# Root of the head norms by ScalarE with a Newton step, fox norm weights in the copies, and query and block-score work inside the last projection group of a hybrid decoder trunk

## Chip, cores and metric

The kernel runs on one core of one Trainium2 chip. The metric is the device time of one execution in microseconds; the time before is the median of 3 runs, 1247.37 us (1247.21 to 1249.06).

## The reference, cut to what matters

The whole program is a two-layer decoder trunk for 256 positions of width 1024 in float32 (attention, dense SwiGLU, gated linear attention, a mixture of 8 experts). The change touches only the first part, between the combined input projection and the attention branches:

```
proj = rmsnorm(x) @ w_in        # 6 column groups: (kc vc ksl kwn) (vsl vwn gates f) qa qb kb vb
qa, ksl, kwn = rope(rmsnorm(head, norm weight))      # per head of 64: x * rsqrt(mean(x^2) + 1e-6) * g
k_cmp = rope(rmsnorm(compress(kc)));  v_cmp = compress(vc)       # 15 blocks
s_c = q . k_cmp / 8 -> softmax -> o_c                # block scores: 15 columns per head
qb, kb = rmsnorm(head, fox norm weight)              # forgetting attention, no rope
cum = cumsum(log_sigmoid(f + bias))                  # added to q.k as two more rows (66 instead of 64)
```

Then follow 18 units of attention (selected, window, fox branch) and the output projection.

## The kernel before

**Input projection.** Weights stream from HBM in units of 4 blocks of 128x512. ScalarE rounds a unit (`split`, L1174), VectorE forms the remainder (`split`, L1498), and TensorE multiplies each block three times (high by high, low, and low by high, L562 to L564) for two tiles of 128 positions. A column group is 8 blocks, that is two units and 48 products. A unit's products wait for VectorE's remainder (`w_lo`), and the next loads and roundings wait until TensorE has used earlier units (`units_used`). Groups alternate between banks 4/5 and 6/7; ScalarE copies each finished group from PSUM to `proj[cg]` with the row norm's root as scale (L1226).

**Order.** There is no planner: every engine has its instruction list written out by hand, and an engine does its list strictly in order. TensorE's list is: groups 0 and 1, turning of the compressed keys (L660), group 2, the 64 products of the compression (L670), turning of keys (L677), group 3, small products (L682, L684), group 4, small products (L691, L695), group 5, then turning of the queries (L706), the cumulative sum of the forget gates (L712 to L714), the block scores (L721, 15 columns each), turning of fox queries and keys (L734), turning of the block probabilities (L738), their products with the values (L742), and the attention loop: scores `qk` (L758, L760), `turn` of the probabilities (L768) and `pv` (L786). In the loop `qk` runs two units ahead.

**Head norms.** VectorE squares a projected group in SBUF (L1534), sums per head (L1535) and signals GpSimd, which computes scale and offset (L498) and raises to the power -0.5 (L499). VectorE then multiplies by the root (L1544) and by the norm weight (L1546) and, for queries and keys, applies the rotation (L1550 to L1553). Between these steps VectorE does unit splits. The compressed key follows the same route on 30 partitions.

**Tail of the preparation.** ScalarE copies turned queries (L1242) and fox rows (L1250) from PSUM, and computes the exponentials of the block scores (L1245); VectorE adds the gate sums (L1692, L1693), masks and normalizes the block scores (L1701 to L1711), copies them (L1715), and scales the block outputs (L1723). The first rowmax (L1730) and exponentials (L1259) of the attention loop come after.

## Time and profile before

| | us |
|---|---|
| median of 3 runs | 1247.37 (1247.21 to 1249.06) |
| span of the profiled execution, first to last instruction | 1243.7 |
| lowest run less that span (the profiled execution's own total is not listed) | 3.5 |
| PE, DVE, ACT, POOL busy in the span | 1225.3, 982.9, 808.2, 52.0 |
| input projection, preparation of attention | 8.8 to 101.1 |
| attention loop up to the output projection | 101.1 to 141.3 |

The profile lists one execution. A timeline row gives the start, the duration from the first to the end of the last instruction of a merged row, engine, source line and operation; TensorE's rows are pipelined, so one more instruction adds less than the duration of one. A row of a chain gives start, duration and the work that held the end at that time. The granted clock is 1.00 for 2.4 GHz and 0.50 for 1.2 GHz.

### The profile page before, as it was taken

Reading aid. Unit: us, or ns where it says so; the run is one execution under the profiler, and the core shown is the slowest. Engines: PE = TensorE matmul, PEld = TensorE weight load, DVE = VectorE, ACT = ScalarE, POOL = GpSimd, SP = SyncE. Lnnn points to the kernel's source line nnn. Section 1 sums busy time; section 2 is a strip of 40 time slices with the busy share of each in tenths; the row PEclk is TensorE's granted clock in tenths of the full one; section 3 lists DMA queues with packets and bytes.
Section 4 is the critical chain, followed back from the end, with each engine's and each line's share of the span. In section 5 each row is a group of like instructions: output and inputs, shape, how many; then the busy total and the mean of one; then the engine's idle time right before and its main releaser. Section 6 shows DMA issues by size and latency. Waiting matters only on the chain.

```text
span 1243.7 us, 16151 instructions
## 1 busy us (share of the span) xinstructions
PE 1225.3 (99%) x6016; PEld 1020.3 (82%) x6021; DVE 982.9 (79%) x945; ACT 808.2 (65%) x877; POOL 52.0 (4%) x52
## 2 busy tenths in 40 slices
PE   8999999999999999999999999999999999999997
PEld 6888888888889886888888888888888888888886
DVE  5887664544567558999889889989989989989896
ACT  6545464343366547777777777777777777777773
POOL 1120000000000001000000000000000000000200
PEclk9989999999999999999999999999999999999999
DMA  9730145544444344999999999999999999999992
GB/s 356 294 135 1 41 163 203 203 173 171 172 184 149 135 153 182 364 401 372 397 377 373 398 376 374 397 380 369 398 381 369 395 384 368 392 371 368 396 422 88
DMA packets 53000, 361.42 MB, mean 291 GB/s; under 512 B 6048, under 2 KB 6560, under 8 KB 10944
## 3 DMA queue, kind: packets, MB, share of 16 engines
q1 hardware_dynamic: 49872, 349.41, 72.7%
q0 software_dynamic: 3056, 11.02, 2.2%
q8 instruction: 50, 0.82, 0.2%
q14 instruction: 22, 0.18, 0.0%
HBM read 354.63 MB, written 5.77 MB: 290 GB/s over the span
## 4 chain that ended last, share of the span: by engine, by line
PE 90%; DVE 4%; DMA 1%; POOL 1%; issue 1%; SPq 1%; ACT 1%; another core or an unknown queue 0%; DVEq 0%
PE bank L564 27%; PE bank L562 27%; PE bank L563 27%; PE bank L1083 2%; DMA raw<-in_weights 1%; PE bank L786 1%; PE bank L758 1%; PE bank L942 1%; DVE low L1498 1%; POOL arena L499 1%; PE bank L768 1%; PE bank L572 1%; PE bank L1048 0%; PE bank L734 0%; PE bank L830 0%
## 5 line engine op out<-in xcount | busy, mean ns | idle before, releaser
L2064 DVE TENSOR_TENSOR low<-raw,whi 128x2048 fp32r<-128x2048 f32 x260 | 594.8, 2291 | 66.5 <-ACT whi L1432 59.2
L1432 ACT CAST whi<-raw 128x2048 fp32r<-128x2048 f32 x260 | 497.4, 1913 | 114.8 <-PE bank L564 114.1
L562 PE MATMUL bank<-whi,hT_hi 128*128 128x512 f32 (+1 forms) x1104 | 430.5, 390 | 1.6 <-DVE low L1567 1.1
L564 PE MATMUL bank<-whi,hT_lo 128*128 128x512 f32 (+1 forms) x1104 | 428.7, 388 | 0.0
L563 PE MATMUL bank<-low,hT_hi 128*128 128x512 f32 (+1 forms) x1104 | 428.1, 388 | 0.0
L562 PEld LDWEIGHTS bank<-whi,hT_hi 128*128 128x128 f32 x1104 | 207.3, 188 | 44.7 <-DVE hT_lo L1516 1.5
L564 PEld LDWEIGHTS bank<-whi,hT_lo 128*128 128x128 f32 x1104 | 207.2, 188 | 42.7
L563 PEld LDWEIGHTS bank<-low,hT_hi 128*128 128x128 f32 x1104 | 207.4, 188 | 41.6
L1498 DVE TENSOR_TENSOR low<-raw,whi 128x2048 fp32r<-128x2048 f32 x67 | 153.0, 2288 | 47.4 <-ACT whi L1174 47.3
L562 PE MATMUL bank<-whi,h_hi 128*128 128x512 f32 x440 | 181.1, 412 | 0.0
L564 PE MATMUL bank<-whi,h_lo 128*128 128x512 f32 x440 | 172.5, 392 | 0.0
L563 PE MATMUL bank<-low,h_hi 128*128 128x512 f32 x440 | 172.0, 391 | 0.0
L1174 ACT CAST whi<-raw 128x2048 fp32r<-128x2048 f32 x67 | 127.9, 1916 | 15.3 <-PE bank L564 10.8
L564 PEld LDWEIGHTS bank<-whi,h_lo 128*128 128x128 f32 x440 | 82.6, 188 | 17.9
L563 PEld LDWEIGHTS bank<-low,h_hi 128*128 128x128 f32 x440 | 83.1, 189 | 14.2
L562 PEld LDWEIGHTS bank<-whi,h_hi 128*128 128x128 f32 x440 | 82.7, 188 | 13.7
L1449 ACT ACTIVATE sg<-bank 128x256 f32<-128x256 f32 x88 | 33.9, 385 | 64.7 <-PE bank L564 64.7
L1282 ACT ACTIVATE sg<-bank,rstd 128x256 f32<-128x256 f32 x22 | 10.4, 474 | 98.4 <-PE bank L564 98.4
L1783 DVE SCALAR_TENSOR_TENSOR hact<-bank,rstd,sg 128x256 f32<-128x256 f32 x22 | 10.6, 484 | 57.7 <-ACT sg L1282 57.7
L1189 ACT ACTIVATE hT_hi<-bank,sml 128x128 fp32r<-128x128 f32 x80 | 22.1, 376 | 29.4 <-PE bank L572 29.4
L2069 DVE TENSOR_TENSOR h_lo<-bank,h_hi 128x256 fp32r<-128x256 f32 x88 | 36.7, 417 | 1.0 <-ACT h_hi L1436 1.0
L2081 DVE TENSOR_TENSOR hact<-sg,bank 128x256 f32<-128x256 f32 x88 | 36.4, 413 | 0.0
(303 smaller groups left out, 830.2 us busy)
## 6 DMA issues: line engine op xcount, KB each, us to landing
raw<-in_weights SPq DMA_DIRECT2D x327, 1024.0 KB, 5.8
sums<-ybuf POOLq DMA_DIRECT2D x7, 512.0 KB, 7.5
arena<-in_compress SPq DMA_DIRECT2D x1, 1088.0 KB, 15.6
x<-in_x SPq DMA_DIRECT2D x2, 512.0 KB, 5.2
raw<-in_weights SPq DMA_DIRECT2D x4, 256.0 KB, 5.7
raw<-in_weights SPq DMA_DIRECT2D x2, 512.0 KB, 7.8
tokens<-hng POOLq DMA_DIRECT2D x2, 512.0 KB, 3.4
out<-x SPq DMA_DIRECT2D x4, 256.0 KB, 3.3
```

What stands on the lines that cost most here:

```text
L562: mm(out_, a_hi, b_hi, start=start, stop=False)
L563: mm(out_, a_hi, b_lo, start=False, stop=False)
L564: return mm(out_, a_lo, b_hi, start=False, stop=stop)
L1083: last = nc.tensor.transpose(bank[2][:, j * P:(j + 1) * P], hact[:, (par + c) % 2, j * P:(j + 1) * P], ident)
L1174: nc.scalar.copy(whi[:, u % SPLIT, :, :], raw[:, u % RAW, :, :]).then_inc(S["w_hi"], 1)
L1189: A(hT_hi[:, k, cols], src[:, j * P:(j + 1) * P], ACT.Copy, scale=sml[:, gc:gc + 1])\
L1432: nc.scalar.copy(whi[:, u % SPLIT, :, :], raw[:, u % RAW, :, :]).then_inc(S["w_hi"], 1)
L1449: A(sg[:, (par + c) % 2, :], bank[(par + c) % 2][:, 0:CH], ACT.Silu).then_inc(S["m_silu"], 1)
L1498: V.tensor_tensor(low[:, u % RAW, :, :], raw[:, u % RAW, :, :], whi[:, u % SPLIT, :, :].bitcast(F32), ALU.subtract).then_inc(S["w_lo"], 1)
L2064: V.tensor_tensor(low[:, u % RAW, :, :], raw[:, u % RAW, :, :], whi[:, u % SPLIT, :, :].bitcast(F32), ALU.subtract).then_inc(S["w_lo"], 1)
L2069: V.tensor_tensor(h2_lo[:, (par + c) % 2, :], bank[2][:, 0:CH], h2_hi[:, (par + c) % 2, :].bitcast(F32), ALU.subtract).then_inc(S["m_h2T"], 1)
L2081: V.tensor_tensor(hact[:, (par + c) % 2, :], sg[:, (par + c) % 2, :], bank[(par + c) % 2][:, CH:2 * CH], ALU.mult).then_inc(S["m_hact"], 1)
```

## The change

- The squares of the head norms are taken by ScalarE from PSUM, with the row root as scale, ahead of the group's copy; VectorE only sums. ScalarE takes the square root (a new function there, which needs another table of functions than the exponential or the logarithm), and VectorE forms the reciprocal and one Newton step in four small instructions, plus one that prepares half of the mean. GpSimd no longer takes part.
- The fox norm weights go as per-partition scale into the copies of the turned rows, so VectorE's second full multiplication for fox queries and keys goes. The last two of the eight fox copies move from ScalarE to VectorE.
- TensorE turns the first half of the queries before group 5, the second half within it (before its block 2), and does cumulative sum, block scores and the turning of fox queries before its block 4. After group 5 remain the turning of fox keys and block probabilities. The products of block probabilities and values come after the scores of attention units 0 and 1.
- VectorE's list is reordered: gates and forget gates earlier, unit splits 10 to 14 at other places; cumulative sum and block scores move to banks 5 and 4.

The diff, cut to its core (waits of `qk` and `turn`, sizes, and the layout of the weights on the host are left out):

```diff
             norm(0)
-            for i, n in enumerate((8, 16, 16, 16)):
-                pool.wait_ge(S["head_ss"], i + 1)
-                inv_root(hrs[:, i, 0:n], hss[:, i, 0:n], HD, n, "head_rstd")
-                if i == 1:
-                    pool.wait_ge(S["kcmp_ss"], 1)
-                    inv_root(hrs[0:30, 4, 0:1], hss[0:30, 4, 0:1], HD, 1, "kcmp_rstd")
...
+                    if hooks is not None and k in hooks:
+                        hooks[k]()
                     if b % UB == 0:
                         pe.wait_ge(S["w_lo"], u0 + b // UB + 1)
...
-            pe.wait_ge(S["headT"], 6)
-            for t in range(NT):
-                for h in range(NH):
-                    g = h // 4
-                    last = mm(bank[6][:, t * P + h * 16:t * P + h * 16 + NCMP], qT[0:HD, h, t * P:(t + 1) * P],
-                              kcmpT[0:HD, g * NCMP:(g + 1) * NCMP], start=True, stop=True)
-            last.then_inc(S["cmp_s"], 1)
-
-            pe.wait_ge(S["aug"], 1)
-            for i in range(8):
+            def later_queries():
+
+                pe.wait_ge(S["vbd"], 1)
+                pe.wait_ge(S["kcmpT"], 1)
+                queries_turned(2)
+                queries_turned(3)
+
+            def fox_turned(i):
+
                 w, t, half = i // 4, i // 2 % 2, i % 2
-                if i % 4 == 0:
-                    pe.wait_ge(S["head_done"], 3 + w)
-                if i >= 4:
-                    pe.wait_ge(S["foxT"], i - 3)
                 for j in range(4):
                     h = half * 4 + j
                     last = nc.tensor.transpose(bank[i % 4][0:66, j * P:(j + 1) * P], faug[:, w, t, h, :], ident)
                 last.then_inc(S["foxT_psum"], 1)
+
+            def block_scores():
+
+                pe.wait_ge(S["proj"], 10)
+                pe.wait_ge(S["fox_lf"], 1)
+                mm(bank[5][:, 0:8], tri, fz[:, 4, 0:8], start=True, stop=True)
+                mm(bank[5][:, 8:16], ones, fz[:, 4, 0:8], start=True, stop=False)
+                mm(bank[5][:, 8:16], tri, fz[:, 4, 8:16], start=False, stop=True).then_inc(S["cum"], 1)
+                pe.wait_ge(S["headT"], 6)
+                for t in range(NT):
+                    for h in range(NH):
+                        g = h // 4
+                        last = mm(bank[4][:, t * P + h * 16:t * P + h * 16 + NCMP], qT[0:HD, h, t * P:(t + 1) * P],
+                                  kcmpT[0:HD, g * NCMP:(g + 1) * NCMP], start=True, stop=True)
+                last.then_inc(S["cmp_s"], 1)
+                pe.wait_ge(S["head_done"], 3)
+                pe.wait_ge(S["aug"], 1)
+                for i in range(4):
+                    fox_turned(i)
+
+            pe.wait_ge(S["head_done"], 2)
+            pe.wait_ge(S["headT"], 2)
+            queries_turned(0)
+            queries_turned(1)
+            in_group(5, {2: later_queries, 4: block_scores})
+            pe.wait_ge(S["head_done"], 4)
+            for i in range(4, 8):
+                pe.wait_ge(S["foxT"], i - 3)
+                fox_turned(i)
             pe.wait_ge(S["cmp_p"], 1)
             for t in range(NT):
-                last = nc.tensor.transpose(bank[7][:, t * P:(t + 1) * P], sc[:, t, :], ident)
+                last = nc.tensor.transpose(bank[5][:, t * P:(t + 1) * P], sc[:, t, :], ident)
             last.then_inc(S["cmp_pT_psum"], 1)
-            pe.wait_ge(S["cmp_pT"], 1)
-            for t in range(NT):
-                mm(bank[4 + t][:, :], pcT[:, t, :], vbd, start=True, stop=True).then_inc(S["cmp_o"], 1)
 
 
...
             pe.wait_ge(S["pool_chain"], 3)
             qk(0)
             qk(1)
+            pe.wait_ge(S["cmp_pT"], 1)
+            for t in range(NT):
+                mm(bank[4 + t][:, :], pcT[:, t, :], vbd, start=True, stop=True).then_inc(S["cmp_o"], 1)
...
+
+            def queries_copied(i):
+
+                t, half = i // 2, i % 2
+                act.wait_ge(S["headT_psum"], 3 + i)
+                nc.scalar.copy(qT[0:HD, half * 4:half * 4 + 4, t * P:(t + 1) * P],
+                               bank[i][0:HD, :].rearrange("p (h n) -> p h n", h=4)).then_inc(S["headT"], 1)
+
+            def fox_copied(i):
+
+                w, t, half = i // 4, i // 2 % 2, i % 2
+                act.wait_ge(S["foxT_psum"], i + 1)
+                A((fqT, fkT)[w][0:66, half * 4:half * 4 + 4, t * P:(t + 1) * P],
+                  bank[i % 4][0:66, :].rearrange("p (h n) -> p h n", h=4), ACT.Copy,
+                  scale=sml[0:66, (R_FQ, R_FK)[w]:(R_FQ, R_FK)[w] + 1]).then_inc(S["foxT"], 1)
+
             for cg in range(A_IN_CG):
                 split(2 * cg + 4)
+                if cg == 3:
+                    head_root(1, 16)
+                if cg == A_IN_CG - 1:
+                    for i in range(4):
+                        fox_copied(i)
+                    act.wait_ge(S["cmp_d"], 1)
+                    A(sc, sc, ACT.Exp, scale=HD ** -0.5).then_inc(S["cmp_e"], 1)
+                    fox_copied(4)
+                    fox_copied(5)
                 w = FRONT_WIDTH.get(cg, BLK)
                 act.wait_ge(S["units_used"], 2 * (cg + 1))
+                if cg == 0:
+                    head_squares(0, 0, 256)
+                if cg == 2:
+                    head_squares(2, 1, 0)
+                if cg == 3:
+                    act.wait_ge(S["head_ss"], 2)
+                    head_squares(3, 2, 0)
+                if cg == 4:
+                    act.wait_ge(S["head_done"], 2)
+                    head_squares(4, 3, 0)
                 for t in range(NT):
                     A(proj[cg][:, t, 0:w], bank[4 + 2 * (cg % 2) + t][:, 0:w], ACT.Copy, scale=rstd[:, t:t + 1])\
                       .then_inc(S["proj"], 1)
+                if cg == 0:
+                    head_root(0, 8)
+                if cg == 4:
+                    queries_copied(0)
+                    queries_copied(1)
                 if cg < A_IN_CG - 1:
                     split(2 * cg + 5)
+                if cg == 3:
+                    act.wait_ge(S["kcmp_ss"], 1)
+                    A(hrs[0:30, 4, 0:1], hss[0:30, 4, 0:1], ACT.Sqrt, scale=1.0 / HD, bias=sml[0:30, R_EPS:R_EPS + 1])\
+                      .then_inc(S["kcmp_sqrt"], 1)
+                    head_root(2, 16)
+                if cg == 4:
+                    queries_copied(2)
+                    queries_copied(3)
+                    head_root(3, 16)
                 if cg == 2:
                     act.wait_ge(S["hid_in"], 1)
...
+                dve.wait_ge(S["squares"], NT * (which + 1))
+                s3 = sq[:, sq_at[which]:sq_at[which] + n * HD].rearrange("p (r d) -> p r d", d=HD)
+                V.tensor_reduce(hss[:, which, 0:n], s3, AX.X, ALU.add).then_inc(S["head_ss"], 1)
+                dve.wait_ge(S["head_ss"], which + 1)
+                link(V.tensor_scalar(hmh[:, which, 0:n], hss[:, which, 0:n], -0.5 / HD, -0.5 * EPS, ALU.mult, ALU.add))
+
+            def sharper(at):
+
+                link(V.reciprocal(hrs[at], hrs[at]))
+                link(V.tensor_tensor(hnw[at], hmh[at], hrs[at], ALU.mult))
+                link(V.tensor_tensor(hnw[at], hnw[at], hrs[at], ALU.mult))
+                link(V.scalar_tensor_tensor(hrs[at], hnw[at], 1.5, hrs[at], ALU.add, ALU.mult))
+
+            def head_roots(nh, which):
+
+                dve.wait_ge(S["head_sqrt"], which + 1)
+                sharper((slice(None), which, slice(0, NT * nh)))
+
+            def rooted(src, nh, which, dst):
+
+                r3 = hrs[:, which, 0:NT * nh].rearrange("p (t h) -> p t h", t=NT)
+                return V.tensor_tensor(dst, src, bc(r3, 3, HD), ALU.mult)
+
...
+            head_sums(NH, 1)
+            dve.wait_ge(S["fox_l"], 1)
+            V.scalar_tensor_tensor(fz[:, 4, :], fz[:, 0, :], 0.0, fz[:, 3, :], ALU.min, ALU.subtract)\
+             .then_inc(S["fox_lf"], 1)
+            dve.wait_ge(S["gate_e"], 1)
+            link(V.tensor_scalar(gat, gat, 1.0, None, ALU.add))
+            link(V.reciprocal(gat, gat))
             dve.wait_ge(S["proj"], 6)
             qa = proj[2][:, :, :].rearrange("p t (h d) -> p t h d", h=NH)
-            head_squares(qa, NH, 1, 2)
-            split(10)
-            link(head_scale(qa, NH, 1, R_QN, qa, 2))
+            head_roots(NH, 1)
+            link(head_scale(qa, NH, 1, R_QN, qa))
+            rope(qa, tab, NH, four(rA, NH), four(rB, NH)).then_inc(S["head_done"], 1)
...
+            dve.wait_ge(S["kcmp_ss"], 1)
+            link(V.tensor_scalar(hmh[0:30, 4, 0:1], hss[0:30, 4, 0:1], -0.5 / HD, -0.5 * EPS, ALU.mult, ALU.add))
+            split(10)
+            head_sums(NH, 2)
+            dve.wait_ge(S["kcmp_sqrt"], 1)
+            sharper((slice(0, 30), 4, slice(0, 1)))
...
             def fox_scale(w):
-                head_scale(fox(w), NH, 2 + w, (R_FQ, R_FK)[w], faug[:, w, :, :, 0:HD], 3 + w).then_inc(S["head_done"], 1)
+
+                src = proj[3 + w][:, :, :].rearrange("p t (h d) -> p t h d", h=NH)
+                dve.wait_ge(S["proj"], 8 + 2 * w)
+                head_roots(NH, 2 + w)
+                rooted(src, NH, 2 + w, faug[:, w, :, :, 0:HD]).then_inc(S["head_done"], 1)
                 V.memset(faug[:, w, :, :, HD + 1 - w:HD + 2 - w], 1.0)
 
-            dve.wait_ge(S["proj"], 8)
-            head_squares(fox(0), NH, 2, 3)
-            split(12)
+            fox_scale(0)
+            split(11)
             dve.wait_ge(S["vrep"], 1)
             V.tensor_tensor(vbd.rearrange("p (h d) -> p h d", h=NH), bc(bank[2][:, 0:HD], 1, NH),
                             bc(cst[:, C_HMASK:C_HMASK + 8], 2, HD), ALU.mult).then_inc(S["vbd"], 1)
             dve.wait_ge(S["kcmpT_psum"], 1)
             V.tensor_copy(kcmpT[0:HD, 0:30], bank[3][0:HD, 256:286]).then_inc(S["kcmpT"], 1)
-            fox_scale(0)
-            dve.wait_ge(S["proj"], 10)
-            head_squares(fox(1), NH, 3, 4)
-
-            dve.wait_ge(S["fox_l"], 1)
-            V.scalar_tensor_tensor(fz[:, 4, :], fz[:, 0, :], 0.0, fz[:, 3, :], ALU.min, ALU.subtract)\
-             .then_inc(S["fox_lf"], 1)
-
-            dve.wait_ge(S["gate_e"], 1)
-            link(V.tensor_scalar(gat, gat, 1.0, None, ALU.add))
-            link(V.reciprocal(gat, gat))
-            split(13)
+            head_sums(NH, 3)
+            split(12)
             fox_scale(1)
-            split(14)
             dve.wait_ge(S["cum"], 1)
-            cum = bank[0][:, 0:16].rearrange("p (t h) -> p t h", t=NT).unsqueeze(3)
+            cum = bank[5][:, 0:16].rearrange("p (t h) -> p t h", t=NT).unsqueeze(3)
             V.tensor_scalar(faug[:, 0, :, :, HD:HD + 1], cum, HD ** 0.5, None, ALU.mult)
             V.tensor_scalar(faug[:, 1, :, :, HD + 1:HD + 2], cum, -HD ** 0.5, None, ALU.mult).then_inc(S["aug"], 1)
+            split(13)
 
...
+            split(14)
+            for i in (6, 7):
+                half = i % 2
+                dve.wait_ge(S["foxT_psum"], i + 1)
+                V.tensor_scalar(fkT[0:66, half * 4:half * 4 + 4, P:2 * P],
+                                bank[i % 4][0:66, :].rearrange("p (h n) -> p h n", h=4), sml[0:66, R_FK:R_FK + 1], None,
+                                ALU.mult).then_inc(S["foxT_late"], 1)
```

## Rows read from the trace of the kernel before

**Rows 1.** Windows: span; busy us of PE, PEld, DVE, ACT, POOL; clock; DMA share; GB/s

```profile
29.20:80.43 51.23, 51.10 (x287) 42.29 (x285) 42.69 (x66) 25.25 (x23) 12.66 (x7) 1.00 0.65 255
...
80.43:104.00 23.57, 21.39 (x137) 18.55 (x137) 17.22 (x32) 13.01 (x37) 3.10 (x2) 0.86 0.12 45
```

**Rows 2.** Waits of the DMA queue on SyncE, 560 to 1230 us: total, times, longest

```profile
SPq L450 <- PE bank L564: 487.4, 222, 3.1
```

**Rows 3.** Timeline of TensorE, 69 to 102 us: start, duration, instruction, count, idle before

```profile
69.39 0.50 PE L562 MATMUL bank<-whi,hT_hi 128*128 128x512 f32 x1
...
80.43 1.91 PE L706 MATMUL bank<-cst,arena 128*64 128x128 f32 x16
82.41 0.39 PE L712 MATMUL bank<-arena,cst 128*128 128x8 f32 x2
...
83.94 5.22 PE L721 MATMUL bank<-arena 64*128 64x15 f32 x32 [0.70 <-ACT arena L1242]
89.57 5.19 PE L734 MATMUL bank<-cst,arena 128*66 128x128 f32 x32 [0.41 <-DVE arena L1693]
94.59 0.38 PE L738 MATMUL bank<-cst,arena 128*128 128x128 f32 x2
95.49 1.98 PE L742 MATMUL bank<-arena 128*128 128x512 f32 x4 [0.52 <-DVE arena L1715]
97.31 2.17 PE L758 MATMUL bank<-arena 66*128 66x128 f32 x16
...
99.53 1.03 PE L758 MATMUL bank<-arena 66*128 66x256 f32 x4
100.40 0.27 PE L760 MATMUL bank<-msk_bits 128*128 128x256 bf16 x1
101.11 0.66 PE L768 MATMUL bank<-cst,arena 128*128 128x128 f32 x4 [0.44 <-ACT arena L1259]
```

**Rows 4.** The chain that ended last, 55 to 103 us: start, duration, what

```profile
55.60 2.19 POOL arena L498
57.86 2.91 POOL arena L499
...
81.70 2.91 POOL arena L499
...
102.74 0.44 PE bank L768 x4
```

**Rows 5.** Windows of the granted clock, columns as in rows 1

```profile
82.41:85.70 3.29, 2.59 (x22) 2.53 (x23) 2.98 (x2) 2.66 (x4) 2.19 (x1) 1.00 0.70 289
85.70:89.20 3.50, 3.46 (x18) 3.35 (x17) 3.46 (x4) 0.00 (x0) 0.00 (x0) 0.52 0.02 5
89.20:92.60 3.40, 3.03 (x15) 2.55 (x16) 2.60 (x11) 1.60 (x4) 0.00 (x0) 0.50 0.00 0
...
41.40:45.20 3.80, 3.74 (x64) 3.77 (x64) 3.80 (x2) 3.02 (x3) 0.00 (x0) 1.00 1.01 418
```

**Rows 6.** Timeline of TensorE, 40.9 to 46 us

```profile
40.94 0.39 PE L564 MATMUL bank<-whi,hT_lo 128*128 128x512 f32 x1
41.46 3.89 PE L670 MATMUL bank<-arena 128*64 128x30 f32 x64
```

**Rows 7.** Timeline of VectorE, the last instruction before the compression's products

```profile
40.96 0.35 DVE L1605 TENSOR_TENSOR arena<-esc,sml 128x120 f32<-128x120 f32 x1
```

**Rows 8.** VectorE by line and shape, 22 to 101 us: busy, mean ns, idle before

```profile
L1498 DVE TENSOR_TENSOR low<-raw,whi 128x2048 fp32r<-128x2048 f32 x13 | 29.5, 2284 | 5.3 <-ACT whi L1174 5.2
...
L1544 DVE TENSOR_TENSOR hn<-arena 128x1024 f32<-128x1024 f32 x3 | 3.7, 1225 | 5.8 <-POOL arena L499 5.8
...
L1709 DVE RECIPROCAL arena<-arena 128x16 f32<-128x16 f32 x1 | 0.2, 245 | 0.0
...
L1711 DVE TENSOR_TENSOR arena<-arena 128x16 f32<-128x16 f32 x1 | 0.2, 178 | 0.0
```

**Rows 9.** ScalarE by line and shape, 22 to 101 us

```profile
L1226 ACT ACTIVATE arena<-bank,rstd 128x512 f32<-128x512 f32 x10 | 6.3, 681 | 13.1 <-PE bank L564 13.1
...
L1245 ACT ACT_TABLE_LOAD x1 | 1.3, 1283 | 0.0
```

More of the change, by code:

```diff
@@ L695, in _, with queries_turned @@
             nc.tensor.transpose(bank[3][0:HD, 256:286], kcm[0:30, 3, :], ident[0:30, 0:30]).then_inc(S["kcmpT_psum"], 1)
-            in_group(5)
-            pe.wait_ge(S["head_done"], 2)
-            pe.wait_ge(S["vbd"], 1)
-            pe.wait_ge(S["kcmpT"], 1)
-            for i in range(4):
+            def queries_turned(i):
                 t, half = i // 2, i % 2
-                if i < 2:
-                    pe.wait_ge(S["headT"], i + 1)
                 for j in range(4):
@@ L788, in pv @@
                 last.then_inc(S["pv"], 1)
-            pe.wait_ge(S["foxT"], 8)
             pe.wait_ge(S["pool_chain"], 3)
@@ L1580, in _ @@
             keys = proj[0][:, :, 256:512].rearrange("p t (h d) -> p t h d", h=4)
-            head_squares(keys, 4, 0, 1)
+            head_sums(4, 0)
             split(5)
@@ L1748, in _ @@
             rowmax(1)
+            for t in range(NT):
+                dve.wait_ge(S["cmp_o"], t + 1)
+                V.tensor_tensor(heads(oacc[:, t, 0:512]), heads(bank[4 + t][:, :]), bc(facc[:, t * 8:t * 8 + 8], 2, HD),
+                                ALU.mult).then_inc(S["o_done"], 1)
             for u in range(AU):
```

94 lines of the change are left out of this document (40 added, 54 removed).

## The prediction

> **What bounds the kernel now.** I read the windows by stage first. While the input groups run, from 29.2 to 80.4 us, TensorE is busy for 51.1 of 51.2 us; in the 23.6 us after it, it is busy for 21.4 at a granted clock of 0.86 [rows 1]. So there are two things to look for: idle time and clock in the tail after group 5, and anything that would open a gap in the groups. Then I read what comes later. SyncE's queue waits for TensorE to free units, 487 us in all from 560 to 1230 us [rows 2]; the stream of weights isn't what holds the long expert stage, TensorE is. A microsecond gained or lost on TensorE before 141 us therefore reaches the end whole. The third view is TensorE's timeline over group 5 and the tail [rows 3]: group 5 starts at 69.39, ends at 80.43, and the first probabilities are turned at 101.11. Those 20.68 us between are the change's target. The chain of waits shows GpSimd's two instructions (2.19 and 2.91 us, later 2.91) on VectorE's way [rows 4], and VectorE idles 5.8 us for them [rows 8]; but TensorE works on through most of that, so their removal by itself is worth little. It lets VectorE be ready early enough for the move on TensorE.
>
> **Part 1, what stays on TensorE.** Tail work, each at 2.4 GHz. Turning the queries: 1.98 us (80.43 to 82.41) [rows 3]. Cumulative sum: 6 instructions at the pace of the turns, 0.11 each (four take 0.44) [rows 4], 0.70. Block scores: 32 instructions from 83.94 to 89.16 (the next row's start less its idle), of which the clock was full only up to about 85.7 [rows 3, 5]; 1.76 plus half of 3.46 gives 3.49. Fox turns: 32 by 0.11, 3.50. Block probabilities turned: 0.24. Scores of units 0 and 1: 97.31 to 99.53, 2.22. Block outputs: 4 instructions from 95.49 to about 97.5, 2.00. Scores of unit 2: 99.53 to 100.67, 1.14 [rows 3]. The sum is 15.27 us against 20.68, so 5.4 us are waits and low clock. About 2.0 of them are the shown waits (0.70, 0.41, 0.52, 0.44), some 0.1 are edges, and 3.4 is the clock, which stood at half for 6.9 us from 85.7 to 92.6 [rows 5].
>
> **Part 2, do the waits go?** I laid the new lists of VectorE and ScalarE out with these durations: a split 2.28, a multiply or sum over 1024 elements 1.22, a reciprocal 0.25 and a small instruction 0.18, with 0.03 between linked ones [rows 8]; a group's copy or square 0.63 on ScalarE from its 6.3 us for 10, a table load 1.28 [rows 9]. VectorE loses three squares of 1.22 and two multiplications by the norm weight of 1.22 each, and gains five Newton chains of 4 instructions, some 0.88 each, five small scalings (0.2 each) and two fox copies (0.68 each, taken from the nearest row, 128x512 elements in PSUM). The root comes back from ScalarE while VectorE does other items. Result: group 5 starts at about 71.1. The compressed keys, which the second half of the queries waits for ahead of block 2, are ready at 72.4 and TensorE comes there at 73.8: slack 1.3 us. The gate sums for the fox turns are ready at 78.6, needed at 81.6. The last part of group 5 needs split 11, done at 71.7, needed at 77.5. Block probabilities: scores end at 81.6, maximum and difference by 83.0, then ScalarE is still in its four fox copies until 84.4, loads the exponential's table (1.28) and finishes at 86.1; VectorE's product at 86.9, needed at 90.6. The copy of the turned probabilities is done at 92.0, needed at 93.0; unit 0's exponentials at 94.5, needed at 96.0. So no wait is left, with the products of the block outputs standing where TensorE used to wait for rowmax and exponentials. ScalarE gains eight squares (5.0 us), four roots with one for the compressed key and two more table loads beyond those shown; it idles 13.1 us ahead of the group copies alone [rows 9], so these cost nothing as long as the order above holds. All new tail work of VectorE and ScalarE hides behind group 5 and the fox turns. GpSimd's part and the smaller constants cost nothing either: no queue of it is touched but its own waits, and no DMA moves.
>
> **Part 3, what the change adds on the path.** (a) In the keys' norm, the root is used only after split 5, and then a chain of reciprocal and three small instructions stands where nothing stood: 0.25 + 3 x 0.21 = 0.85 us. Behind it on VectorE are the keys' rotation, the key copies and the block additions, the last of which ends at 41.31 [rows 7] and releases the compression's 64 products at 41.46; TensorE's previous product (started 40.94, 0.23 after the one before it) was through at 41.17 [rows 6]. There is no slack, so 0.85 us of TensorE is lost. Bounds: 0 (if the chain overlapped) and 1.3. I take 0.85. (b) Group 5 is cut twice, once more by turns ahead of it. The first product after turns shows 0.50 against 0.39 [rows 3, 6]. For two more edges, 0.2.
>
> So without the clock: 5.4 - 0.85 - 0.2 = 4.35 us less.
>
> **Part 4, the clock.** The narrow products (8 and 15 columns) began at 82.41; the clock fell to its lower level at about 85.7, stayed there while 32 instructions went without a gap, and rose at 92.6, 3.0 us after the wide turns (128 columns) had begun at 89.57 [rows 3, 5]. In the new order the narrow stretch is shorter, 0.70 + 3.49 = 4.2 us instead of 6.8, without the 0.8 us gap, and between wide products. The compression's 64 products (30 columns, 3.8 us) passed at full clock [rows 5, 6]. Bounds for the loss: 0 if it behaves as the compression, 3.45 if as before. In length 4.2 lies near 3.8, but with half its columns. I take 1.0 us, a short dip at the end of the scores, nearer to the row it resembles in length. The same worry holds for the compression itself, which now follows a gap of about 1.1 us instead of 0.3.
>
> A rule speaks here. The Trainium skill, TensorE: Matmul & The Clock Gate, in its section on HAM oscillation, tells of a clock that drops when idle gaps open between matmuls and advises keeping them together. By that rule the new stretch, which has no gap, would lose nothing. The trace agrees only in part: a gap of 0.8 us came first, but at the lower level TensorE was busy for 3.46 of 3.50 us, and stayed low.
>
> **Sum.** 4.35 - 1.0 = 3.35 us. The profiled execution spans 1243.7 us; the runs lie 3.5 to 5.4 above that, and with the lowest two of the three it stands for about 1247.3, the median. 1247.4 - 3.4 = **1244.0 us**.
>
> **Rivals.**
> *No fall at all.* The wide work on both sides holds the clock. For it: the compression's row. Against: 15 columns, where the engine mostly loads weights. Time 1247.4 - 4.35 = 1243.0. Chance 0.27.
> *The fall as before*, inside group 5: it sets in 3.3 us after narrow work begins, as before, and the following wide products run at 1.2 GHz until 3 us after; by that pacing some 4.8 us low, 2.4 lost, by the whole old price 3.45. Time 1245.4 to 1246.5. Chance 0.2.
> *A second fall at the compression*, by the longer gap ahead of it, with up to 3.45 us on top of the forecast: 1245.5 to 1247.4. Chance 0.08. The windows around 41 to 45 us show 1.00 now, with a gap of 0.3.
> *Slower: VectorE's linked chains make TensorE wait within group 5.* Place: ahead of block 2, TensorE waits for `kcmpT`, which on VectorE stands behind two Newton chains, split 10, the fox sum, the compressed key's chain, the fox chain and split 11. TensorE's list is strict, so all later group products stand behind this wait, and with them the units to be freed. The slack is 1.3 us. Between 54 and 72 us stand some 17 small linked instructions; if each handover took 0.21 longer than 0.03 (the sum of ScalarE's round trips included), they would be 3.6 later, the wait 2.3 us, the first chain 1.7 rather than 0.85, and a gap of that size ahead of narrow products would bring the whole fall of 3.45. That is 5.4 - 1.7 - 0.2 - 2.3 - 3.45 = -2.3: 1249.7. It decides when more than 1.3 us are added there, and becomes slower than before from about 1 us beyond that together with the fall. Against it: linked small instructions in this trace follow each other by 0.03, in every place. Chance 0.05.
> *The change doesn't do what it says*: the tail's waits only move to the first units of the loop (a rowmax, the two late fox copies) since VectorE holds 1.0 us of slack there. Then 1 to 2 us more: 1245 to 1246. Chance 0.05, in which I include the rest.
>
> **Numbers.** Forecast 0.35, its own spread 1243.4 to 1244.9. The range for 8 in 10 takes in no fall with a cheaper first chain below (1242.3) and the whole fall above (1246.5). A measurement of this kernel can tell about 0.2%, 2.5 us, from no change: the border is 1244.9. Faster: nearly all of the forecast and of the first rival, 0.62. Same: most of the others, 0.32. Slower 0.06, the slower rival and a bad second fall.
>
> **What would show it.** Right if, after, the first turned probabilities come 4 to 5 us earlier than 101.11 less the dip; if the products of the compression start 0.8 later than 41.46 behind VectorE's last block addition; if group 5 with its inserts runs without idle; if the timeline shows the block outputs between the scores of units 1 and 2 and no idle before the first turn of probabilities; and if windows over the block scores show a clock between 0.5 and 1.0 for a short stretch. Wrong if TensorE idles before the second half of the queries (chains too slow), before the turning of block probabilities (ScalarE's order or tables), or if ScalarE's split of a unit comes so late behind a wait for a head sum that a group's products wait for their remainder. It would also be wrong if time beyond 141 us changed, where nothing was edited.

## The result, and the profile after

The changed kernel takes **1253.12 us** (median of 4 runs, 1252.75 to 1253.38) against 1247.72 of the kernel before beside it (4 runs, 1247.21 to 1249.06): ratio 1.0046, 95% interval 1.0033 to 1.0058. It is slower by 5.4 us in the medians and 5.7 by the ratio, outside the range of the forecast and on the side that was given 0.06. The profiled execution took 1252.75 us with a span of 1250.9, so 1.85 lies around the span; the span of before was 1243.7, which is 7.2 less.

The windows of the changed kernel, TensorE alone (start and end, length, busy us and instructions, granted clock, DMA share, GB/s):

```profile
29.20:80.40 51.20, 49.86 (x275) 0.93 0.59 233
80.40:104.00 23.60, 23.54 (x148) 0.93 0.27 90
40.00:50.00 10.00, 8.66 (x80) 0.75 0.78 320
50.00:60.00 10.00, 10.00 (x41) 0.91 0.25 92
81.60:85.40 3.80, 3.80 (x34) 1.00 0.82 276
85.40:89.60 4.20, 4.20 (x20) 0.59 0.02 4
```

Against [rows 1] the second stretch is what was wanted: busy 23.54 of 23.60 us, clock 0.93 rather than 0.86. The first stretch is the opposite: 1.3 us of idle time, where there had been 0.1, and a clock of 0.93 where it was 1.00. The next two rows place it at 40 to 53 us. The timeline of TensorE, from the compression to the first turned probabilities:

```profile
40.84 0.39 PE L561 MATMUL bank<-whi,hT_lo 128*128 128x512 f32 x1
42.56 4.94 PE L669 MATMUL bank<-arena 128*64 128x30 f32 x64 [1.34 <-DVE arena L1685]
47.43 1.92 PE L676 MATMUL bank<-cst,arena 128*64 128x128 f32 x8
...
50.00 0.63 PE L561 MATMUL bank<-whi,hT_lo 128*128 128x512 f32 x1
...
73.05 0.65 PE L690 MATMUL bank<-arena,cst 15*128 15x64 f32 x4
...
77.34 1.03 PE L700 MATMUL bank<-cst,arena 128*64 128x128 f32 x8
...
81.64 3.74 PE L730 MATMUL bank<-arena 64*128 64x15 f32 x32
85.31 2.98 PE L716 MATMUL bank<-cst,arena 128*66 128x128 f32 x16
...
98.40 1.88 PE L809 MATMUL bank<-arena 128*128 128x512 f32 x4
...
101.09 0.60 PE L782 MATMUL bank<-cst,arena 128*128 128x128 f32 x4
```

Three things are to be seen. The compression's 64 products start 1.1 us later than in [rows 6], after a gap of 1.34, and last 4.94 instead of 3.89; the turns behind them take 1.92 for 8, and group products 0.63 each instead of 0.39: a fall of the clock. The small products L690 start at 73.05. In the same view of the kernel before their like is

```profile
68.78 0.65 PE L691 MATMUL bank<-arena,cst 15*128 15x64 f32 x4
```

so 4.3 us were lost by then. From there to the first turned probabilities it is 28.0 us, against 32.3 before. The tail gained 4.3 us, and the compression had taken them beforehand: the first turned probabilities start at 101.09, at 101.11 before [rows 3].

So the first 101 us come out even, and the 7.2 us of the span are lost later, in lines that the change does not touch. I compared the starts of the same products in both traces. The FFN's hidden turns are late by 0.0 at their first and 1.4 at their last; through the gated stage (365 to 428 us) it stays at 1.5; over the experts it grows again. Their hidden turns, before (L1083) and after (L1099), by all instructions of one line:

```profile
L1083 PE MATMUL bank<-cst,hact x176: 270/271/301, 497.3 to 1229.0; 128*128 128x128 f32 x176
```

```profile
L1099 PE MATMUL bank<-cst,hact x176: 270/271/273, 498.7 to 1236.7; 128*128 128x128 f32 x176
```

1.4 us late at the first and 7.7 at the last. The page's groups of instructions show which products grew (busy, mean ns), first before, then after:

```profile
L562 PE MATMUL bank<-whi,h_hi 128*128 128x512 f32 x440 | 181.1, 412 | 0.0
L564 PE MATMUL bank<-whi,h_lo 128*128 128x512 f32 x440 | 172.5, 392 | 0.0
L563 PE MATMUL bank<-low,h_hi 128*128 128x512 f32 x440 | 172.0, 391 | 0.0
```

```profile
L559 PE MATMUL bank<-whi,h_hi 128*128 128x512 f32 x440 | 183.1, 416 | 0.0
L561 PE MATMUL bank<-whi,h_lo 128*128 128x512 f32 x440 | 174.5, 397 | 0.0
L560 PE MATMUL bank<-low,h_hi 128*128 128x512 f32 x440 | 174.2, 396 | 0.0
```

These are the second products of FFN and experts, whose other operand is `h2_hi` or `h2_lo`: 4, 5 and 5 ns more each, 14 ns times 440 = 6.2 us. The products with `hT_hi` and `hT_lo` grew a little too: from 560 to 1230 us those with `low` went from 389 to 390 ns and those with `hT_lo` from 389 to 391, 627 of each, another 1.9 us. The code of both kinds is unchanged. What did change is where `h2_hi` and `h2_lo` lie. The diff shortens the tile of small constants `sml` from 550 to 426 columns (2208 and 1728 bytes in each partition, rounded up to 32), and each tile in SBUF is placed behind the one before it. By the addresses of the compiled programs `h2_hi` started 86,528 bytes behind `whi` before, which is 338 x 256; now it starts 480 bytes lower, 32 past a multiple of 256.

### The profile page after: what moved, and what is told of

It is laid out like the page before. It is cut to its first block, busy times and chain, and to the rows that moved or that the text cites. A ratio compares the mean times of both kernels' runs of the same rounds, so it can differ in the third digit from the quotient of the medians.

```text
span 1250.9 us, 16182 instructions
## 1 busy us (share of the span) xinstructions
PE 1233.9 (99%) x6016; PEld 1021.7 (82%) x6021; DVE 982.4 (79%) x966; ACT 817.2 (65%) x891; POOL 36.5 (3%) x42
## 3 DMA queue, kind: packets, MB, share of 16 engines
q1 hardware_dynamic: 49872, 349.34, 72.4%
## 4 chain that ended last, share of the span: by engine, by line
PE 94%; DVE 2%; DMA 1%; SPq 1%; issue 1%; ACT 0%; DVEq 0%
PE bank L561 28%; PE bank L559 28%; PE bank L560 28%; PE bank L1099 2%; DMA raw<-in_weights 1%; PE bank L770 1%; PE bank L800 1%; PE bank L958 1%; PE bank L782 1%; PE bank L569 1%; PE bank L1064 0%; PE bank L669 0%; PE bank L846 0%; PE bank L716 0%; PE bank L1056 0%
```

## The experiments

**Theories.** P: the place of the tiles in SBUF costs what is lost beyond 101 us. F: the change itself costs it (other order of engines, another phase of the weights' stream), and the place is chance. For the early part, N: the Newton chain ahead of the keys' scaling delays the compression, and the gap brings the fall of the clock.

**Constants padded to their old width** (e1), the changed kernel:

```
-        sml = sb("sml", [P, R_END])
+        sml = sb("sml", [P, R_END + 124])
```

> The whole change, with the constants tile padded back to its old width (550 instead of 426 columns), so that every tile behind it lies at its address of before, a multiple of 64 bytes, instead of 32 bytes off. Theory A (the place of the tiles costs the time that shows after 101 us, where nothing was edited): products with h_hi and h_lo go back from 416, 396, 397 ns to 412, 391, 392 ns, the expert stage from 497 to 1229 us takes 6 us less, and the median is 1253.1 - 7 = 1246 us. Rival B (it comes from what the edited part left behind, in queues, clock or weight supply): no difference, 1253 us.

Measured: 1243.85 us (12 runs, 1242.76 to 1247.74), ratio to before 0.998 [0.997, 0.9989]. From 560 to 1230 us the products with `h2` are back at 412, 391 and 392 ns, and those with `hT` at 389. The same change with its tiles where they were is faster than before by 2.5 us.

**The other way round: the kernel before, tiles moved by 32 bytes** (e2):

```
-        ctx.enter_context(nc.sbuf_tensor("line_pad", [P, 8], F32))
+        ctx.enter_context(nc.sbuf_tensor("line_pad", [P, 16], F32))
```

> The kernel before, with only the small pad ahead of the arena made 32 bytes longer, so that the arena and all tiles behind it lie 32 bytes off a multiple of 64; no instruction differs. Theory A: 1247.7 + 7 = 1254.7 us, with the loss in the stages with h_hi and h_lo. Rival B: 1247.7 us.

Measured: 1253.92 us (6 runs), ratio 1.0056 [1.0042, 1.007], products at 416, 396 and 397 ns. 32 bytes of unused memory in the kernel before cost 7.4 us in the medians, more than the 5.4 by which the changed kernel is slower. P stands and F falls.

**The keys' Newton step, scaling and rotation ahead of split 5** (e3, on top of e1):

```
             head_sums(4, 0)
-            split(5)
             dve.wait_ge(S["const_in"], 16)
             ...
             rope(keys, tab, 4, four(rA, 4), four(rB, 4)).then_inc(S["head_done"], 1)
+            split(5)
```

> e1 with the keys' Newton chain, scaling and rotation ahead of unit split 5 on VectorE, into its 3.5 us of idle. Theory C (the gap that the chain opened ahead of the compression's products, 1.34 us, brought on the low clock over them): the compression starts at 41.2 without a gap, the clock stays full over it, and the time is 4 us below e1 (1.3 gap, about 2.7 of clock), 1242 us. Rival D (narrow products lower the clock by themselves, whatever stands ahead): only the gap goes, 1.3 us below e1, 1244.7 us.

Measured: 1241.35 us (6 runs, 1240.39 to 1243.19), ratio 0.9953 [0.9938, 0.9968]. Timeline of TensorE:

```profile
40.78 0.39 PE L561 MATMUL bank<-whi,hT_lo 128*128 128x512 f32 x1
41.10 3.10 PE L669 MATMUL bank<-arena 128*64 128x30 f32 x50
...
77.06 4.19 PE L730 MATMUL bank<-arena 64*128 64x15 f32 x32
81.18 3.62 PE L716 MATMUL bank<-cst,arena 128*66 128x128 f32 x16
...
98.11 0.60 PE L782 MATMUL bank<-cst,arena 128*128 128x128 f32 x4
```

No gap is left and the compression passes at full clock. The first turned probabilities start 3.0 us earlier than in e1 (101.07). So N holds in this: with the chain out of the way both the gap and the fall are gone, here and in the traces of e8 and e18, which carry the same edit. The gain is 2.5 us in the medians, where 4 was expected. One reason is in the traces. The fall at the scores is deeper here: windows of the granted clock in e1, then in e3:

```profile
84.00:88.00 4.00, 4.00 (x30) 0.80 0.38 158
80.00:84.00 4.00, 4.00 (x33) 1.00 0.35 109
```

```profile
84.00:88.00 4.00, 4.00 (x14) 0.62 0.00 0
80.00:84.00 4.00, 4.00 (x22) 0.52 0.21 86
```

A second reason is likely but not shown: the fall at the compression may not come in every execution of e1. The one with a trace, which has it, is among 5 of 12 with a mean clock of 0.993 to 0.995 and spans of 1243.3 to 1245.9; the other 7 have 0.996 or 0.997 and spans around 1241.7, and no trace. The 6 runs of e3 lie all at 0.996 to 0.998.

**The block scores (with cumulative sum and the fox queries' turns) behind group 5** (e4, on top of e1):

```
-            in_group(5, {2: later_queries, 4: block_scores})
+            in_group(5, {2: later_queries})
+            block_scores()
```

> e1 with cumulative sum, block scores and fox query turns after group 5 instead of ahead of its block 4 (the queries still before and within it). If the place within the group is what hides ScalarE's and VectorE's chain: the maximum, the table load, the exponentials and the masks come to lie on the path, about 3 to 4 us more than e1, 1249.5 us. Rival (the products had room anyway, the queries' place is what matters): within 1 us of e1.

Measured: 1250.21 us (10 runs, 1246.3 to 1253.51), ratio 1.0026 [1.0012, 1.004]; 6.4 us above e1, twice what was expected. The waits of the tail are back in TensorE's timeline, and the clock is low through most of the turns (6.32 us for 32; 0.50 from 88 to 92 us and up again by 94):

```profile
84.19 4.37 PE L730 MATMUL bank<-arena 64*128 64x15 f32 x32
88.49 6.32 PE L716 MATMUL bank<-cst,arena 128*66 128x128 f32 x32
95.52 0.44 PE L750 MATMUL bank<-cst,arena 128*128 128x128 f32 x2 [0.70 <-DVE arena L1789]
...
99.74 1.98 PE L810 MATMUL bank<-arena 128*128 128x512 f32 x4 [1.56 <-DVE arena L1803]
```

This execution took 1247.25; 7 of the 10 took 1249.7 or more, at a mean clock of 0.991 to 0.993, and where it fell in those isn't shown. The three others lie about 3 us above e1's seven quickest, which is what was expected. So without the insertion into group 5 the change is slower than the kernel before. Its other parts (GpSimd's removal, the weights in the copies, the later block outputs) were not taken out one by one.

**The kernel before with a chain of four linked small instructions ahead of the keys' scaling** (e7):

```
+            dve.wait_ge(S["head_rstd"], 1)
+            link(V.reciprocal(hss[:, 5, 0:8], hss[:, 0, 0:8]))
+            link(V.tensor_tensor(hss[:, 5, 8:16], hss[:, 0, 0:8], hss[:, 5, 0:8], ALU.mult))
+            link(V.tensor_tensor(hss[:, 5, 8:16], hss[:, 5, 8:16], hss[:, 5, 0:8], ALU.mult))
+            link(V.scalar_tensor_tensor(hss[:, 5, 0:8], hss[:, 5, 8:16], 1.5, hss[:, 5, 0:8], ALU.add, ALU.mult))
             link(head_scale(keys, 4, 0, R_KN, keys, 1))
```

> The kernel before with four linked small instructions (the shapes of the Newton chain, on a row nothing reads) ahead of the keys' scaling on VectorE. Theory C: the compression's products start about 0.85 us later and the low clock comes over them in part of the runs: 0.85 to 2.5 us more, 1247.4 to 1249.0 us. Rival D (the gap does nothing to the clock): 0.85 us more in every run, 1247.4 us. Rival (the chain is hidden there): 1246.5 us.

Measured: 1247.46 us (12 runs), ratio 1.0013 [0.9999, 1.0026]. In the profiled execution (span 1245.4) the gap is there, and yet the clock stays up: the 64 products take 3.89 us and the turns 1.06, as in [rows 6]:

```profile
42.82 3.89 PE L670 MATMUL bank<-arena 128*64 128x30 f32 x64 [1.09 <-DVE arena L1610]
46.64 1.06 PE L677 MATMUL bank<-cst,arena 128*64 128x128 f32 x8
```

4 of its 12 runs have a mean clock of 0.992 and spans of 1249.6 on average, against 1245.1 for 8 at 0.996 or 0.997. Where in these 4 the clock fell isn't shown, since the trace is of another execution. Nor is it shown that the chain brought it: of the 23 runs of the kernel before beside it 2 had such a low clock (0.993, spans of 1247.9 and 1250.4), and so had 3 of 10 runs of e12 below, which has no chain. The price of the chain alone, 0.3 us in the spans of the quiet runs and 0.7 in the medians, is within the noise too.

There are twenty traces: before, changed and eighteen experiments, of which e8 to e18 are described below. Together they say more than these two. The next lines are from e12 and e15, which are the kernel before with some tiles moved and not one instruction added:

```profile
41.79 4.99 PE L671 MATMUL bank<-arena 128*64 128x30 f32 x64 [0.78 <-DVE arena L1606]
41.58 4.59 PE L671 MATMUL bank<-arena 128*64 128x30 f32 x64 [0.41 <-DVE arena L1606]
```

| gap ahead of the compression, us | traces | the 64 products took over 4 us, the clock fell |
|---|---|---|
| none shown, 0.23 or 0.30 | 9 (before, e2, e3, e5, e6, e8, e13, e17, e18) | 0 |
| 0.41 to 0.78 | 5 (e9, e10, e12, e14, e15) | 2 (e12, e15) |
| 1.09 | 2 (e4, e7) | 0 |
| 1.23 to 1.45 | 4 (the changed kernel, e1, e11, e16) | 4 |

So the fall goes with a gap, not with its length alone, and the kernel before, with tiles moved, had it in an execution with a gap of 0.41 us. What decides between the two outcomes from 0.41 to 1.09 us isn't shown.

**Fox turns alternated with the block scores** (e8, on top of e3), to keep the narrow products from standing alone:

```
                 for t in range(NT):
                     for h in range(NH):
+                        if t * NH + h >= 3:
+                            turn_next()
                         ...
```

> e3 with the turning of the fox queries mixed between the block scores, one turn of 128 columns after each score from the fourth on, instead of behind all of them. If the unbroken row of 15-column products is what lowers the clock within group 5: the clock stays at 1.00 over group 5 and the time falls by what the low stretch costs, 2 to 3 us, to about 1239 us; the scores end 1.7 us later, which the block probabilities' slack of about 4 us takes. Rival (any stretch with few columns lowers it, mixed or not, or the later scores reach the path): no gain, 1241.4 us or more.

Measured: 1247.05 us (11 runs), ratio 1.0002 [0.9993, 1.0011], 5.7 above e3: a miss. The timeline shows why:

```profile
80.79 0.39 PE L744 MATMUL bank<-arena 64*128 64x15 f32 x2
81.11 0.30 PE L731 MATMUL bank<-cst,arena 128*66 128x128 f32 x1
81.35 0.39 PE L744 MATMUL bank<-arena 64*128 64x15 f32 x2
81.67 0.30 PE L731 MATMUL bank<-cst,arena 128*66 128x128 f32 x1
```

A score is two instructions of 15 columns. A score and a turn come every 0.55 us at full clock, and the turns don't hold the clock: behind 82 us the same pattern takes 0.89, and the clock stands at 0.50 from 82.4 to 92.2 us.

**What about the tiles' place costs?** First the two parts of the shift by themselves, in the kernel before:

```
+        sb("pad_a", [P, 8])
         h2_hi = sb("h2_hi", [P, 2, CH], F32R)
         h2_lo = sb("h2_lo", [P, 2, CH], F32R)
+        sb("pad_b", [P, 8])
```

is e5, which moves h2 by 32 bytes and what follows by 64. e6 has `pad_a` and a `line_pad` of `[P, 16]`: arena, sg and hact by 32, h2 and what follows by 64.

> The kernel before with 32 bytes of pad ahead of h2_hi and 32 behind h2_lo: only these two tiles, the stationary operands of the 1320 down products, lie 32 bytes off a multiple of 64. Theory A1 (their place is the whole price): the full 7 us of the shifted kernel, 1253.5 us, and the products with h_hi and h_lo at 416, 396, 397 ns. Rival A2 (the price is spread over the arena, the activation buffers and the picks): 1 to 3 us, with these products at 412, 391, 392 ns.

> The counterpart: the arena, sg and hact lie 32 bytes off, h2_hi, h2_lo and all behind them are back on multiples of 64. Theory A1: as before, 1246.5 us. Rival A2: most of the 7 us, 1250 us or more.

Measured: e5 1251.88 us, ratio 1.0038 [1.0025, 1.0051]; e6 1253.23, 1.0057 [1.0044, 1.007]. Read as starts off a multiple of 64 bytes this made no sense, as the one part cost two thirds of the whole and the other all of it. But e6 had also moved h2, by 64 bytes. The next four took that apart, still in the kernel before except e11:

```
-        ctx.enter_context(nc.sbuf_tensor("line_pad", [P, 8], F32))
+        ctx.enter_context(nc.sbuf_tensor("line_pad", [P, 24], F32))
```

is e9, everything from arena on by 64 bytes. e10 has only `pad_a`, with `[P, 16]`: h2 and what follows by 64. e11 is the changed kernel with a `line_pad` of `[P, 16]`. e12 has only `pad_b`: what follows h2, by 32.

> The kernel before, with all tiles from arena on moved up by 64 bytes: every start keeps its distance to a multiple of 64 bytes. If a start off a multiple of 64 is what costs (theory M), the time is that of before, 1246 to 1248 us, and the products of the expert stage with h2_hi and h2_lo last 412, 391 and 392 ns. If any move against the tiles that stay (whi, low, sml) costs (rival R), it is 1251 to 1254 us and they last 416 to 418, 395, 396 ns.

> The kernel before, with h2_hi, h2_lo and all behind them moved up by 64 bytes while arena, sg and hact stay: this is what the two one-sided shifts had in common (picks and all behind it lay 64 bytes further in both). Theory M expects no change, 1246 to 1248 us. If the place of picks and what follows, or the distance between hact and h2, is what costs (rival R2), 1251 to 1254 us and 395 to 396 ns.

> The changed kernel with line_pad 64 bytes instead of 32, so that arena and all behind it start at a multiple of 64 again, while wa2, esc and the other small tiles between sml and line_pad stay 32 bytes off. If the arena and the tiles of the loops are what matters, the time is that of the aligned version, 1243 to 1246 us. If the small tiles carry part of the price, 1248 to 1252 us.

> The kernel before, with only picks and all behind it (y_hi, y_lo, disp, combT, ybuf, mtab) moved up by 32 bytes, while arena, sg, hact, h2_hi and h2_lo stay. None of these is read or written in the unit loops of the experts' products. Theory M, by which a product or an activation of the loops pays for its own operands' place, expects 1246 to 1248 us. If the place of the tiles behind h2_lo is what costs, 1250 to 1254 us.

Measured, ratios to before: e9 1.0052 [1.0035, 1.007], e10 1.006 [1.0042, 1.0079], e11 1.0037 [1.0024, 1.0049], e12 1.0007 [0.9996, 1.0017]. Multiples of 64 are no help, a move of the tiles behind h2 by 32 bytes costs nothing clear of noise, a move of h2 does. So larger steps, `sb("pad_a", [P, n])` ahead of h2_hi with n of 32, 64 and 128:

> The kernel before, with h2_hi, h2_lo and all behind them moved up by 128 bytes, where 64 cost 6 to 8 us and moving the tiles behind h2_lo alone cost nothing. In the kernel before, low, whi, hT_hi, hT_lo and h2 all start 128 bytes past a multiple of 512. Theory M128, a start off a multiple of 128 bytes costs: 1246 to 1248 us, h products 411, 391, 392 ns. Theory D, the distance to the weights' tiles must be a multiple of 256 or 512, or any move costs: 1251 to 1255 us, 417, 395, 395 ns.

> The same with 256 bytes. M128 expects 1246 to 1248 us; a distance of 256 as the unit expects the same; a distance of 512 as the unit, or any move at all, 1251 to 1255 us.

> The same with 512 bytes. M128, 256 and 512 as the unit all expect 1246 to 1248 us. If only the very place of before is fast (a unit larger than 512 bytes, or an accident of the timing), 1251 to 1255 us.

Measured: 128 bytes 1250.41 us, 1.003 [1.0019, 1.0042]; 256 bytes 1246.63, 1.0001 [0.9991, 1.001]; 512 bytes 1246.86, 1.0001 [0.9991, 1.001]. Windows of 560 to 1230 us by line and shape, of e10 (64 bytes) and then of e14 (256 bytes):

```profile
L563 PE MATMUL bank<-whi,h_hi 128*128 128x512 f32 x314 | 130.9, 417 | 0.0
L565 PE MATMUL bank<-whi,h_lo 128*128 128x512 f32 x315 | 124.5, 395 | 0.0
L564 PE MATMUL bank<-low,h_hi 128*128 128x512 f32 x315 | 124.5, 395 | 0.0
```

```profile
L563 PE MATMUL bank<-whi,h_hi 128*128 128x512 f32 x317 | 130.5, 412 | 0.0
L565 PE MATMUL bank<-whi,h_lo 128*128 128x512 f32 x316 | 123.9, 392 | 0.0
L564 PE MATMUL bank<-low,h_hi 128*128 128x512 f32 x316 | 123.6, 391 | 0.0
```

Of the steps tried, 32, 64 and 128 bytes cost time and 256 and 512 don't, so the unit is 256 bytes. A step of 128 costs half of what 64 does, less than theory D expected. Is it the start, or the distance to the other tiles that TensorE reads? In e17 a pad of 128 bytes ahead of the first tile moves everything in the kernel before. In e16 the changed kernel gets 224 bytes (`[P, 56]`) ahead of h2_hi alone, and e18 is e16 with the edit of e3:

> The kernel before with every tile, the weights' tiles and hT too, moved up by 128 bytes: all distances stay, all starts that TensorE reads are now multiples of 256 instead of 128 past one. If the distance between h2 and the weights' or hT tiles is what counts: 1246 to 1248 us. If the start itself is (128 past a multiple of 256): 1250 us or more, and the hT products, 389 ns before, grow too.

> The changed kernel with 224 bytes ahead of h2_hi alone, so that h2_hi and h2_lo lie a multiple of 256 bytes (337 x 256) from whi again, while arena, sg, hact and all small tiles stay where the change put them. If the place of h2 is the whole price: the aligned version's time, 1243 to 1245 us, h products 411, 391, 392 ns. If the other tiles carry some of it: 1246 to 1251 us.

> The same with the keys' Newton step, scaling and rotation ahead of split 5. Expected at the time of e3 (1241 us; 1240 to 1243), which had the tiles placed by padding the constants; 2 to 4 us below e16.

| kernel | h2 to whi, past a multiple of 256 | ratio to before |
|---|---|---|
| e17, all by 128 | 0 | 0.9999 [0.9989, 1.0008] |
| e16, changed kernel | 0 | 0.9998 [0.9987, 1.001] |
| e18, changed, keys early | 0 | 0.9977 [0.9968, 0.9986] |
| e13 | 128 | 1.003 [1.0019, 1.0042] |
| e10 | 64 | 1.006 [1.0042, 1.0079] |
| e5 | 32 | 1.0038 [1.0025, 1.0051] |

With all distances kept, a start moved by 128 bytes costs nothing (the products with hT stay at 389 ns): it is the distance. In e9 arena, sg and hact moved along with h2 and the time was lost all the same; in e16 the small tiles behind `sml` stayed where the change put them and most of it came back. So what counts is the distance to tiles that lie from the start of memory up to `sml`. `low`, `whi`, `hT_hi`, `hT_lo` and the constants keep their distances to each other in every run, so `whi` in the table stands for all of them: which one counts isn't separated. Correcting h2 alone takes the changed kernel from 1.0046 to 0.9998, 6.0 us of it. The rest up to e1's 0.998 is 2.2 us, with 2.7 to 3.0 between e18 and e3 (0.9977, 0.9953) the same size. e16's rows show part of it: 415 ns for the product of `whi` with `h_hi`, 411 or 412 where all lies as before, 3 to 4 ns by 440, 1.3 to 1.8 us:

```profile
L560 PE MATMUL bank<-whi,h_hi 128*128 128x512 f32 x316 | 131.2, 415 | 0.0
```

Which tile that still lay elsewhere (arena, sg, hact or the small ones) does this wasn't tried.

## Why the prediction was wrong, by its steps

**The step that failed** is the last sentence of Part 2, "the smaller constants cost nothing either: no queue of it is touched but its own waits, and no DMA moves". I priced the shorter tile as instructions and transfers and didn't see that it moves every tile behind it. It cost 8.2 us (1.0046 against 0.998 of e1, the same kernel with the tile at its old width), three times the gain. The prediction did say that it "would also be wrong if time beyond 141 us changed, where nothing was edited"; that is where it changed. No rival had this mechanism. The slower one (VectorE's chains making TensorE wait within group 5) did not happen: from 70 to 96 us the windows show TensorE busy throughout.

**Part 1, the waits and the clock of the tail: right in kind, and its total by two errors that met.** 5.4 less 0.2 for edges less 1.0 for the dip is 4.2; measured from the small products to the first turned probabilities it is 4.3. But the dip cost 1.7, not 1.0. The other 0.8 is in the sum of the work that remains, which was too long: turning the queries takes 0.82 and 0.79 from its start to the next product, not 1.98 in all; the block outputs take 1.71, not 2.00; the scores of unit 2 take 0.98, not 1.14. So waits and low clock were 6.2 rather than 5.4, and 6.2 - 0.2 - 1.7 = 4.3. The order in the timeline is the one laid out by hand: block outputs between the scores of units 1 and 2, no idle before the turn.

**Part 2, slack: right.** TensorE came to the second half of the queries at 77.34 without waiting, and the compressed keys were ready at 76.00: slack 1.3 us, as worked out, though both came later than foretold (73.8 and 72.4) by the fall at the compression. In e3, without that fall, it is 72.76 and 71.41, the same slack. No wait in the tail is left. That GpSimd's removal is what made this possible is argued; no run keeps GpSimd in the new order.

**Part 3 (a): right in place, short in size.** 0.85 was expected. The chain starts at 33.79 and the scaling behind it at 34.62, where it stood at 33.47 before: 1.15, of which 0.83 are the four instructions and the rest is that the list ahead of them ended 0.3 later. The chain of waits:

```profile
33.79 0.20 DVE arena L1605
34.02 0.18 DVE arena L1606
34.22 0.18 DVE arena L1607
34.41 0.18 DVE arena L1608
34.62 0.70 DVE hn L1618
```

**The second fall at the compression** was a rival with 0.08, and it came on top of the forecast in the profiled execution: 4.3 us lost up to the small products, 1.1 by the start and most of the rest, 3.2, by the clock, within the 3.45 given. Of the five traces of the changed order with the keys' chain in its place (the changed kernel, e1, e4, e11, e16) four have it, so 0.08 was far too low. An edit in VectorE's order (e3) removes it. A row for it was at hand: the only fall of that trace came after a gap, of 0.70 us by [rows 3] (the prediction says 0.8). A single trace of before hid the other half, that the kernel before, with nothing but tiles moved, has this fall too in some executions (e12, e15).

**Part 4, the dip at the scores: right in kind, too small.** The clock held from 81.6 to 85.4 and stood at 0.59 for the 4.2 us behind, which costs 4.2 x (1 - 0.59) = 1.7 by its clock, against 1.0 taken and 3.45 as the bound. In e3 it was deeper still: 0.52 and 0.62 over 8 us cost 3.4 us by the same reckoning, the whole old price. The rule of the Trainium skill (TensorE: Matmul & The Clock Gate, HAM oscillation) that ties the drop to idle gaps would have given nothing here, as there was none; the trace shows a fall all the same, behind narrow products without a gap. At the compression the fall goes with a gap, as the table above shows, but gaps of 1.09 us passed without one in e4 and e7.

**The level.** I set the span of 1243.7 against the median of 1247.37. Every run that lists both has 1.8 to 2.4 us around its span, so that execution took some 1245.6, near the fastest of before; two single traces can differ by 2 to 3 us through a fall that one of them has.

Taken together: 1244.0 was forecast for the change without any move of tiles, and e1, which is that, measures 1243.85, partly by luck: the level was too high, the work that remains too long, the dip too small and the fall at the compression left out, and these errors met. The forecast for the kernel as it is was wrong by 9 us.

## What to carry to other kernels

A change of one tile's size moves all tiles behind it, and that alone can cost more than the change brings: print the addresses of both versions, and hold the distances between the tiles that TensorE reads (here a multiple of 256 bytes between h2 and those at the start) with a pad, before a time is read as the worth of an edit. Where time appears in lines that nobody edited, look at the means of the same products in both profiles. The best version measured is e3, the change with the tiles held and the keys' chain ahead of a split: 1241.35 us, 0.9953 of before.

## What the runs showed of the hardware that was not expected

- With the stationary operands h2_hi and h2_lo at a distance off a multiple of 256 bytes from the weights' tile (and the tiles beside it), their products of 128x512 take 1 to 6 ns longer in the mean of some 400, whichever of 32, 64 or 128 bytes it is off; 64 cost the most in time (1.006), 128 the least (1.003), and the interval of 32 (1.0038) overlaps both. The products with hT, which didn't move, take up to 2 ns longer in the same runs, so it isn't a product's own operand alone. The Trainium skill (SBUF — State Buffer, Operand start alignment) gives the element's size as the rule and says it is about legality, not speed; all pads here are multiples of 32 bytes and keep that rule, and speed depended on the place all the same (e2, e10, e13 against e14 to e17). The mechanism isn't shown.
- Ahead of 64 products of 30 columns, gaps of 0.41 to 1.09 us were followed by the low clock in two traces of seven, gaps of 1.23 us and more in four of four, and no gap or one up to 0.30 in none of nine. Runs of one kernel differ by some 4.5 us with the mean clock (e7: 0.992 in 4 of 12, 0.996 or 0.997 in 8), so a single profile can mislead; the mean clock that goes with each run helps to see it.
- Two 15-column instructions (one score) and a 128-column turn in alternation take 0.55 us at full clock (e8). By rows of before, at 0.11 for each of the three instructions, they would take 0.33.
